# Convolution stage of a two-block decoder kernel: the input normed ahead of its projection, the depthwise taps dealt anew over three engines

## The chip, the cores and the metric

The kernel runs on one core of one Trainium2 chip. The metric is the device time of one execution in microseconds (us), lower is better. A core has five engines that run beside each other, each with a queue of its own: PE (TensorE, matrix products into the eight banks of PSUM), DVE (VectorE, elementwise), ACT (ScalarE, functions and scaled copies), POOL (GpSimd, elementwise on SBUF only) and SP (which here only starts transfers). They meet at semaphores.

## The reference, cut to what matters

A model of three layers is computed for 512 tokens and 1024 channels in float32. The change lies in the first half of the first layer, a convolution module:

```python
def conformer_conv(h, w_pw1, b_pw1, w_dw, b_dw, ln_g, ln_b, w_pw2, b_pw2):
    u = h @ w_pw1 + b_pw1                 # 1024 -> 2048; h = rmsnorm(x, norm_mix[0])
    a, gate = jnp.split(u, 2, axis=-1)
    u = a * jax.nn.sigmoid(gate)
    u = lax.conv_general_dilated(         # causal, 31 taps, each channel for itself
        u, w_dw[:, None, :], window_strides=(1,), padding=[(CONV_WIDTH - 1, 0)],
        dimension_numbers=("NWC", "WIO", "NWC"), feature_group_count=CONV_CHANNELS) + b_dw
    u = jax.nn.silu(layernorm(u, ln_g, ln_b))
    return u @ w_pw2 + b_pw2
```

Behind it follow the gated feed-forward, attention and retention layers, which the change leaves as they are.

## The kernel before

**Tiles.** Channels lie on the 128 partitions, tokens along the free side: `X`, `U` and `CV` are eight tiles (m = 0 to 7) of 128x512. Every weight matrix streams through in units of 256 columns. A float32 unit `W_raw` is split into a rounded part `W_hi` (ACT) and a rest `W_lo` (DVE), and so is the input (`H_hi`, `H_lo`); a product is then three matmuls, lines L627, L628 and L629. The first layer `pw1` has eight units j = 0 to 7 of 8 x 2 products, 48 matmuls each; two units are in flight, in PSUM banks PS0/PS1 and PS2/PS3. Unit j gives one tile of the linear half and one of the gate, and from them DVE makes tile j of `U`.

**The norm.** `H_hi` and `H_lo` hold x times its gain, without the token's factor 1/rms. ACT squares the tiles of `X`, DVE adds the squares up in `SSUM`, PE sums over the partitions (`first_sum`, L686) after three products of unit 1, ACT takes the root, DVE the reciprocal `R4`, PE spreads it over a bank (`token_spread`, L692), ACT copies it to `R`, and every unit's results are multiplied by `R` on DVE (`T_g`, `T_u`; L1970, L1973) before gate and product (`U`, L1976).

**The 31 taps of eight tiles, 248 in all.** PE takes 66 (tile 1, parts of 5 and 7) as three matmuls each with a diagonal matrix of tap weights (`D_hi`, `D_lo`, built on ACT by `diagonals` in chunks of six taps, three chunks ahead). 32 of them stand among the products of units 4 to 7, the rest behind unit 7. They need the tile's split input `UP_hi`, `UP_lo`. DVE takes 124 (tiles 0, 3, 4, 6), one instruction each (L1930), counted out behind each unit by `DVE_TAPS`. POOL takes 58 (tile 2, parts of 5 and 7): ACT writes tap weight times shifted `U` to one of four `TAP` buffers (`scaled_tap`, L1272), and POOL adds it to `CV` (L1752). Each addition waits for the one before, since both go into the same tile. DVE joins the parts of split tiles (`conv_join`).

**Order.** Every engine's order is written by hand. Among PE's taps stand the three products of `bias_products` (L715), which make the attention's bias table. They wait for two small DMAs and for a memset of `table` by POOL (L1774, semaphore `pads_set` at 2). POOL reaches it between its second and third tile:

```python
            taps(1)
            mean_add(3)
            mean_add(4)
            pool.wait_ge(ln_sum, len(MEAN_POOL) - 1)
            pool.wait_ge(acc_ready, 2 * (L.base + L.n))
            nc.gpsimd.memset(table[BUCKETS:BUCKETS + 1, :], NEG).then_inc(pads_set, 1)
            pool.wait_ge(pads_set, 2)
            taps(2)
```

Once all tiles are made, PE sums them over channels (L772 to L778), DVE subtracts the mean (L1997), and the layernorm and layer `pw2` follow.

Of the kernel before, what the change touches and what calls it, by code (L numbers as in the profile page):

```python
# [5 lines left out]
F32 = mybir.dt.float32  # L6
# [4 lines left out]
P = 128  # L11
# [31 lines left out]
SS_ADDS = [7, 7, 7, 7, 7, 5, 7, 5]  # L43
# [6 lines left out]
COPIED_NORMS = [MIX0, FFN_PRE, FFN_POST]  # L50
# [19 lines left out]
POOL_TAPS = [(m, t) for m, end in POOL_TILES for t in range(end)]  # L70
POOL_ENDS = [n + 1 for n, (m, t) in enumerate(POOL_TAPS) if (m, t + 1) in POOL_TILES]
SCALED = [n for n, (m, t) in enumerate(POOL_TAPS) if t]
CHUNK = 6
CHUNKS = (len(PE_TAPS) + CHUNK - 1) // CHUNK
FIRST_TAP, TAPS_INSIDE = 64, 32
CHUNK_AT = {g: c for c, g in enumerate([40, 46, 52] + [FIRST_TAP + 2 * CHUNK * (c - 2) for c in range(3, 8)])}
TAKE_AT = FIRST_TAP + 2 * PE_ENDS[0] + 1
SCALED_AT = [50 + 3 * k // 2 for k in range(30)] + [101 + 3 * k // 2 for k in range(18)]
MEAN_POOL = [0, 2, 3, 1, 4]
MADE = [0, 3, 4, 5, 6, 7]  # L80
# [103 lines left out]
def build(nc, a, out):  # L184
# [13 lines left out]
    with ctx:  # L198
# [99 lines left out]
        TAP = [SQ[:, 0, :], SQ[:, 1, :], STD[:], T_hid[:]]  # L298
# [3 lines left out]
        D_hi = [sb(f"D_hi{i}", [P, CHUNK, P], F32R, at=w_at + 11264 * i + 8192) for i in range(3)]  # L302
        D_lo = [sb(f"D_lo{i}", [P, CHUNK, P], F32R, at=w_at + 11264 * (3 + i) + 8192) for i in range(3)]
        tap_hi = sb("tap_hi", [P, CONV_WIDTH * DT], F32R, at=arena + 68352)
# [70 lines left out]
        acc_free = sem("acc_free")  # L375
        x_ready = sem("x_ready")
# [20 lines left out]
        glu_made = sem("glu_made")  # L397
# [122 lines left out]
        def _(sp):  # L520
# [38 lines left out]

            sp.dma_start(vecs[:, 0:DT], a["vecs"][:, 0:DT]).then_inc(gain_in, 16)  # L560
            sp.dma_start(W_raw[0][:, 0:FIRST_COLS], a["pw1"][0][:, 0:FIRST_COLS]).then_inc(first_in, 16)
            for i in range(4):
                sp.dma_start(X[:, 2 * i:2 * i + 2, :], a["x"][:, 2 * i:2 * i + 2, :]).then_inc(x_in[i], 16)
                if i == 0:
                    sp.dma_start(W_raw[0][:, FIRST_COLS:2 * FIRST_COLS], a["pw1"][0][:, FIRST_COLS:2 * FIRST_COLS]).then_inc(raw_in[0], 16)
# [50 lines left out]
        def _(pe):  # L616
# [65 lines left out]
            def first_sum():  # L682

                pe.wait_ge(ss_made, SS_ADDS[MIX0])
                for b in range(4):
                    last = nc.tensor.matmul(AUX[0][:, b:b + 1], tokens(SSUM, b), ones[:, 0:1], start=(b == 0), stop=(b == 3))  # L686
                last.then_inc(stat_ready, 1)
# [30 lines left out]
            def conv_tap(n):  # L718
# [6 lines left out]
                if n in (0, *PE_ENDS):  # L725
                    pe.wait_ge(u_lo, p + 1)
                    pe.wait_ge(r_copied, COPIED_NORMS.index(MIX0) + 1)
                    if p == 2:
                        pe.wait_ge(conv_pe_taken, 1)
                if x == 0:  # L730
                    pe.wait_ge(diag_made, c + 1)
                d_hi, d_lo = D_hi[c % 3][:, x, :], D_lo[c % 3][:, x, :]
# [5 lines left out]
            L = layers["pw1"]  # L738
            for k in range(L.kt):
# [9 lines left out]
            for j in range(1, L.n):  # L749
# [3 lines left out]
                for half in range(2):  # L753
                    for k in range(L.kt):
                        last = product(j % 2, L.kt, half, k, H_hi, H_lo)
                        if k == L.kt - 1:
                            last.then_inc(acc_ready, 1)
                        g = SLOTS * j + 8 * half + k
                        if g == SUM0_AT:
                            first_sum()  # L760
                        if g == SPREAD0_AT:
                            pe.wait_ge(r_made, MIX0 + 1)
                            token_spread(AUX[1], r_ps)
# [9 lines left out]
            pe.wait_ge(conv_made, MADE.index(5) + 1)  # L773
            nc.tensor.matmul(PS[0][:], ones, CV[:, 5, :], start=False, stop=False)
            pe.wait_ge(conv_made, MADE.index(6) + 1)
            nc.tensor.matmul(PS[0][:], ones, CV[:, 6, :], start=False, stop=False)
            pe.wait_ge(conv_made, MADE.index(7) + 1)
            nc.tensor.matmul(PS[0][:], ones, CV[:, 7, :], start=False, stop=True).then_inc(ln_sum_ready, 1)  # L778
# [394 lines left out]
        def _(act):  # L1173
            act.dma_start(cmat[:, 0:2, :], a["cmat"][:, 0:2, :]).then_inc(const_in, 16)
            act.wait_ge(gain_in, 16)
# [55 lines left out]

            warm_table(ACT.Sqrt)
            act.wait_ge(first_in, 16)
            nc.scalar.activation(W_hi[0][:, 0:FIRST_COLS], W_raw[0][:, 0:FIRST_COLS], ACT.Copy).then_inc(w_half, 1)
            for m in range(0, DT, 2):
                if m == 2:
# [1428 lines left out]
```

## Time and profile before

| | |
|---|---|
| time, median of 3 runs | 1810.86 us (1808.42 to 1811.15) |
| the profiled execution | 1810.43 us, of it span 1808.7 us |
| PE busy | 1743.7 us (96%) |
| DVE, ACT, POOL busy | 1017.8, 716.0, 249.1 us |
| first matmul of `pw1` | 9.61 us |
| PE's longest pause in the stage | 12.1 us, up to 141.99 us |
| first instruction of the layernorm (L1997) | 170.60 us |

The span goes from the first to the last instruction; 1.73 us of the time lie outside it. Times in the trace are counted from the start of the span. The convolution stage ends at 170.60 us; all that follows hangs on that point and is the same program in both kernels. A matmul's own duration (0.39 us) overlaps the next one; what it takes of PE is the distance from one start to the next.

### The profile page before, as it was taken

Reading aid. Unit: us, or ns where it says so; the run is one execution under the profiler, and the core shown is the slowest. Engines: PE = TensorE matmul, PEld = TensorE weight load, DVE = VectorE, ACT = ScalarE, POOL = GpSimd, SP = SyncE. Lnnn points to the kernel's source line nnn. Section 1 sums busy time; section 2 is a strip of 40 time slices with the busy share of each in tenths; the row PEclk is TensorE's granted clock in tenths of the full one; section 3 lists DMA queues with packets and bytes.
Section 4 is the critical chain, followed back from the end, with each engine's and each line's share of the span. In section 5 each row is a group of like instructions: output and inputs, shape, how many; then the busy total and the mean of one; then the engine's idle time right before and its main releaser. Section 6 shows DMA issues by size and latency. Waiting matters only on the chain.

```text
span 1808.7 us, 20938 instructions
## 1 busy us (share of the span) xinstructions
PE 1743.7 (96%) x7984; PEld 1385.3 (77%) x7984; DVE 1017.8 (56%) x1268; ACT 716.0 (40%) x1064; POOL 249.1 (14%) x183
## 2 busy tenths in 40 slices
PE   7987899999999999999999999989999999999997
PEld 6874788888888777788888888756557778888886
DVE  6898664423444556654434434559856677537753
ACT  5776532312233344432212233464554454324431
POOL 0783110000001000100000004572200200000001
PEclk9998899999999999999999999999999899999998
DMA  5220322322232311222322232423202122322221
GB/s 182 70 70 11 115 93 93 119 99 73 98 120 75 121 71 53 86 95 93 128 70 93 96 125 82 146 75 112 80 32 78 62 93 101 119 70 93 101 97 47
DMA packets 28052, 164.62 MB, mean 91 GB/s; under 512 B 4511, under 2 KB 5675, under 8 KB 11596
## 3 DMA queue, kind: packets, MB, share of 16 engines
q1 hardware_dynamic: 25088, 158.11, 25.1%
q10 hardware_dynamic: 2892, 5.55, 1.0%
q8 instruction: 46, 0.75, 0.2%
q14 instruction: 26, 0.21, 0.0%
HBM read 156.28 MB, written 4.47 MB: 89 GB/s over the span
## 4 chain that ended last, share of the span: by engine, by line
PE 80%; DVE 10%; POOL 5%; ACT 3%; issue 2%; DMA 0%; POOLq 0%; DVEq 0%; SPq 0%; ACTq 0%
PE PS L627 25%; PE PS L628 25%; PE PS L629 25%; POOL CV L1752 4%; DVE PS L1930 2%; DVE W_lo L1880 2%; ACT W_hi L1169 1%; DVE WK L2320 1%; DVE SSUM L2361 1%; DVE TOP L2318 1%; PE PS L1060 1%; PE PS L1071 1%; POOL ISC L1824 1%; DVE PS L2497 0%; DVE X L2500 0%
## 5 line engine op out<-in xcount | busy, mean ns | idle before, releaser
L627 PE MATMUL PS<-H_hi,W_hi 128*128 128x512 f32 x1600 | 641.6, 401 | 17.8 <-DVE H_lo L1860 13.5
L629 PE MATMUL PS<-H_hi,W_lo 128*128 128x512 f32 x1600 | 626.0, 391 | 0.0
L628 PE MATMUL PS<-H_lo,W_hi 128*128 128x512 f32 x1600 | 625.8, 391 | 0.0
L1169 ACT ACTIVATE W_hi<-W_raw 128x2048 fp32r<-128x2048 f32 (+2 forms) x130 | 262.6, 2020 | 674.7 <-PE PS L629 674.7
L627 PEld LDWEIGHTS PS<-H_hi,W_hi 128*128 128x128 f32 x1600 | 301.9, 189 | 105.5 <-issue 41.1
L1880 DVE TENSOR_TENSOR W_lo<-W_raw,W_hi 128x2048 fp32r<-128x2048 f32 (+2 forms) x130 | 332.3, 2556 | 59.4 <-ACT W_hi L1169 59.1
L629 PEld LDWEIGHTS PS<-H_hi,W_lo 128*128 128x128 f32 x1600 | 301.8, 189 | 64.5
L628 PEld LDWEIGHTS PS<-H_lo,W_hi 128*128 128x128 f32 x1600 | 302.2, 189 | 58.9 <-issue 1.2
L627 PE MATMUL PS<-HID_hi,W_hi 128*128 128x512 f32 x640 | 250.7, 392 | 7.5 <-DVE HID_lo L2016 7.4
L1727 POOL TENSOR_TENSOR SSUM<-SSUM,SQ 128x512 f32<-128x512 f32 x43 | 63.6, 1480 | 1353.7 <-ACT SQ L1211 1352.3
L629 PE MATMUL PS<-HID_hi,W_lo 128*128 128x512 f32 x640 | 250.0, 391 | 0.0
L628 PE MATMUL PS<-HID_lo,W_hi 128*128 128x512 f32 x640 | 249.9, 391 | 0.0
L627 PEld LDWEIGHTS PS<-HID_hi,W_hi 128*128 128x128 f32 x640 | 120.8, 189 | 34.1 <-issue 8.5
L629 PEld LDWEIGHTS PS<-HID_hi,W_lo 128*128 128x128 f32 x640 | 120.7, 189 | 25.3
L628 PEld LDWEIGHTS PS<-HID_lo,W_hi 128*128 128x128 f32 x640 | 120.9, 189 | 24.8
L2058 DVE TENSOR_TENSOR T_u<-PS,R 128x512 f32<-128x512 f32 x44 | 30.4, 691 | 156.1 <-PE PS L629 156.1
L2066 DVE TENSOR_TENSOR T_hid<-T_u,T_act 128x512 f32<-128x512 f32 x66 | 45.7, 693 | 81.1 <-ACT T_act L1410 78.5
L2031 DVE TENSOR_TENSOR X<-X,PS 128x512 f32<-128x512 f32 x40 | 27.0, 684 | 113.9 <-PE PS L629 113.7
L1930 DVE SCALAR_TENSOR_TENSOR PS<-U,vecs,PS 128x512 f32<-128x512 f32 x112 | 75.5, 752 | 0.2
L1418 ACT ACTIVATE HID_hi<-T_hid 128x512 f32 (+1 forms) x66 | 42.0, 636 | 57.7 <-DVE T_hid L2066 57.7
L1860 DVE SCALAR_TENSOR_TENSOR H_lo<-X,vecs,H_hi 128x512 fp32r<-128x512 f32 x40 | 36.2, 914 | 27.3 <-ACT H_hi L1196 27.2
L2072 DVE TENSOR_TENSOR HID_lo<-T_hid,HID_hi 128x512 f32 (+1 forms) x66 | 45.2, 684 | 1.4 <-ACT HID_hi L1418 1.4
(300 smaller groups left out, 1493.5 us busy)
## 6 DMA issues: line engine op xcount, KB each, us to landing
W_raw<-in_inp SPq DMA_DIRECT2D x13, 1024.0 KB, 4.8
W_raw<-in_pw SPq DMA_DIRECT2D x11, 1024.0 KB, 4.8
W_raw<-in_gu0a SPq DMA_DIRECT2D x11, 1024.0 KB, 4.8
W_raw<-in_gu0b SPq DMA_DIRECT2D x11, 1024.0 KB, 4.8
W_raw<-in_gu1a SPq DMA_DIRECT2D x11, 1024.0 KB, 4.8
W_raw<-in_gu1b SPq DMA_DIRECT2D x11, 1024.0 KB, 4.8
W_raw<-in_gu2a SPq DMA_DIRECT2D x11, 1024.0 KB, 4.8
W_raw<-in_gu2b SPq DMA_DIRECT2D x11, 1024.0 KB, 4.7
```

The lines of the kernel that those rows point to most:

```text
L627: nc.tensor.matmul(dst[:], wh, x_hi[:, k, :], start=(k == first), stop=False)
L628: nc.tensor.matmul(dst[:], wh, x_lo[:, k, :], start=False, stop=False)
L629: return nc.tensor.matmul(dst[:], wl, x_hi[:, k, :], start=False, stop=(k == last))
L1169: nc.scalar.activation(W_hi[b][:, 0:n], W_raw[b][:, 0:n], ACT.Copy).then_inc(w_hi, 1)
L1418: nc.scalar.activation(dst, T_hid[:], ACT.Copy).then_inc(hid_hi_made, 1)
L1727: nc.gpsimd.tensor_tensor(SSUM[:], SSUM[:], SQ[:, m.parity, :], ALU.add).then_inc(ss_made, 1)
L1752: nc.gpsimd.tensor_tensor(CV[:, m, :], CV[:, m, :], TAP[k % len(TAP)], ALU.add).then_inc(pool_tap, 1)
L1860: nc.vector.scalar_tensor_tensor(out=dst, in0=src, scalar=scale, in1=hi, op0=ALU.mult, op1=ALU.subtract).then_inc(h_lo_made, 1)
L1880: nc.vector.tensor_tensor(W_lo[b][:, 0:n], W_raw[b][:, 0:n], W_hi[b][:, 0:n].bitcast(F32), ALU.subtract).then_inc(w_lo, 1)
L1930: i = nc.vector.scalar_tensor_tensor(out=dst, in0=src, scalar=w, in1=acc, op0=ALU.mult, op1=ALU.add)
L2066: nc.vector.tensor_tensor(T_hid[:], T_u[:], T_act[:], ALU.mult).then_inc(hid_made, 1)
L2072: nc.vector.tensor_tensor(HID_lo[:, k, :].rearrange("p o n -> p (o n)"), T_hid[:], hi, ALU.subtract).then_inc(hid_lo_made, 1)
```

## The change

Six things are altered, all up to the layernorm.

1. **The norm goes first.** `X` is loaded before the weights, over two queues. ACT squares it. PE sums each squared tile as it comes (`first_sums`, 8 x 4 products with one column), in place of DVE's additions and `first_sum`. Root, reciprocal and spread follow, then DVE multiplies `X` by the spread factor into `CV` (`normed`), and `H_hi` and `H_lo` are made of that. Only then does unit 0 begin.
2. **Gates from PSUM.** Sigmoid reads the gate's bank, the product the other bank; the two multiplications by `R` per unit are gone.
3. **Order of PE.** All eight units run without taps between them, then 54 taps: tile 4 whole, tile 6 from tap 8. `bias_products` stands behind tap 24, not 55.
4. **POOL's tiles.** 1 and 5 whole, 6 up to tap 7. Each has two sums, `CV` and a new tile `CV2`, taken in turn, so that an addition waits for the one before the last; one more addition joins them.
5. **Buffers.** Eleven `TAP` buffers for four, four chunks of diagonals for three.
6. **DVE** takes tiles 0, 2, 3 and 7 (again 124 taps), 12 behind each of units 0 to 6 and 40 behind unit 7.

```diff
-PE_TILES = [(1, 0), (5, 22), (7, 5)]
+PE_TILES = [(4, 0), (6, 8)]
-DVE_TILES = [0, 3, 4, 6]
-DVE_TAPS = [5, 8, 9, 16, 16, 16, 16]
-POOL_TILES = [(2, CONV_WIDTH), (5, 22), (7, 5)]
+DVE_TILES = [0, 2, 3, 7]
+DVE_TAPS = [12] * 7
+POOL_TILES = [(1, CONV_WIDTH), (5, CONV_WIDTH), (6, 8)]
+PRODUCTS_WITH = [0, 8, 7, 7, 7, 8, 8, 8]
+CHUNKS_WITH = {0: [0, 1], 2: [2], 4: [3]}
...
+            def first_sums():
+
+                for m in range(DT):
+                    pe.wait_ge(sq_made, m + 1)
+                    for b in range(4):
+                        last = nc.tensor.matmul(AUX[0][:, b:b + 1], tokens(FIRST_SQ[m], b), ones[:, 0:1],
+                                                start=(m == 0 and b == 0), stop=(m == DT - 1 and b == 3))
                 last.then_inc(stat_ready, 1)
...
             L = layers["pw1"]
+            first_sums()
+            pe.wait_ge(r_made, MIX0 + 1)
+            token_spread(AUX[1], r_ps)
...
-                        if g >= FIRST_TAP and g % 2 == 0:
-                            conv_tap((g - FIRST_TAP) // 2)
-            for n in range(TAPS_INSIDE, len(PE_TAPS)):
+            for n in range(len(PE_TAPS)):
                 conv_tap(n)
-                if n == 55:
+                if n == 24:
                     bias_products()
...
+            for j in range(L.n):
+                glu_gate(j)
+                if j < L.n - 1:
+                    split_hi(act, L, At(j))
+                scaled_taps(PRODUCTS_WITH[j] // 2)
+                if j - 1 in (4, 6):
+                    conv_hi((j - 1) // 2 - 2)
+                for c in CHUNKS_WITH.get(j, []):
+                    diagonals(c)
+                scaled_taps(PRODUCTS_WITH[j] - PRODUCTS_WITH[j] // 2)
...
-                    pool.wait_ge(pool_tap, n)
-                    nc.gpsimd.tensor_tensor(CV[:, m, :], CV[:, m, :], TAP[k % len(TAP)], ALU.add).then_inc(pool_tap, 1)
+                    pool.wait_ge(pool_tap, n - 1)
+                    nc.gpsimd.tensor_tensor(acc, acc, TAP[k % len(TAP)], ALU.add).then_inc(pool_tap, 1)
...
             taps(1)
             mean_add(3)
-            mean_add(4)
             pool.wait_ge(ln_sum, len(MEAN_POOL) - 1)
             pool.wait_ge(acc_ready, 2 * (L.base + L.n))
             nc.gpsimd.memset(table[BUCKETS:BUCKETS + 1, :], NEG).then_inc(pads_set, 1)
...
+            def normed(m):
+
+                if m == 0:
+                    dve.wait_ge(r_ps, TOKEN_NORMS.index(MIX0) + 1)
+                nc.vector.tensor_tensor(CV[:, m, :], X[:, m, :], AUX[1][:], ALU.mult).then_inc(xn_made, 1)
...
+            normed(0)
+            normed(1)
             dve.wait_ge(w_half, 1)
             nc.vector.tensor_tensor(W_lo[0][:, 0:FIRST_COLS], W_raw[0][:, 0:FIRST_COLS],
                                     W_hi[0][:, 0:FIRST_COLS].bitcast(F32), ALU.subtract).then_inc(first_lo, 1)
...
-                nc.vector.tensor_tensor(T_g[:], PS[2 * b + 1][:], R[:], ALU.mult).then_inc(gate_in, 1)
...
-                nc.vector.tensor_tensor(T_u[:], PS[2 * b][:], R[:], ALU.mult).then_inc(acc_free, 1)
...
-                nc.vector.scalar_tensor_tensor(out=U[:, j, HALO:HALO + SEQ], in0=T_u[:], scalar=vec("b_pw1", j),
-                                               in1=T_act[:], op0=ALU.add, op1=ALU.mult).then_inc(glu_made, 1)
+                nc.vector.scalar_tensor_tensor(out=U[:, j, HALO:HALO + SEQ], in0=PS[2 * (j % 2)][:], scalar=vec("b_pw1", j),
+                                               in1=GATE[j % 2][:], op0=ALU.add, op1=ALU.mult).then_inc(glu_made, 1)
```

The names in the rows of the programs below carry buffer numbers: `PS0` to `PS3` are the units' banks, `PS4` is `AUX[0]`, `PS5` is `AUX[1]`, `SQ`, `T_g`, `T_u`, `T_act`, `T_hid` and `R` hold squares at first and tap products later, and `cmat` holds the constant matrices. What stands in brackets is what an instruction waits for.

On PE the statistics of the norm stood inside unit 1, the sum first:

```order
L628 MATMUL PS2<-H_lo_51,W_hi1_55 128x512
L629 MATMUL PS2<-H_hi_50,W_lo1_57 128x512
L686 MATMUL PS4<-cmat_58,SSUM_64 128x1 [waits ss_made]
L686 MATMUL PS4<-cmat_58,SSUM_64 128x1 x3
L627 MATMUL PS2<-H_hi_50,W_hi1_55 128x512
```

Now PE's program begins with them, one group for each squared tile:

```order
L691 MATMUL PS4<-cmat_58,SSUM_64 128x1 [waits sq_made,const_in]
L691 MATMUL PS4<-cmat_58,SSUM_64 128x1 x3
L691 MATMUL PS4<-cmat_58,SQ_65 128x1 [waits sq_made]
L691 MATMUL PS4<-cmat_58,SQ_65 128x1 x3
...
L691 MATMUL PS4<-cmat_58,R_62 128x1 [waits sq_made]
L691 MATMUL PS4<-cmat_58,R_62 128x1 x3
L698 MATMUL PS5<-cmat_58,R4_72 128x128 [waits r_made]
L698 MATMUL PS5<-cmat_58,R4_72 128x128 x3
```

Four one-column matmuls became 32, and they and the spread stand ahead of the first dense product.

Further down on PE, behind unit 7, the bias products now stand after tap 24, the first tap of the fifth chunk of diagonals:

```order
L739 MATMUL PS4<-UP_hi_141,D_lo3_150 128x512
L737 MATMUL PS4<-UP_hi_141,D_hi0_143 128x512 [waits diag_made]
L738 MATMUL PS4<-UP_lo_142,D_hi0_143 128x512
L739 MATMUL PS4<-UP_hi_141,D_lo0_147 128x512
L721 MATMUL PS1<-onehot_101,table_102 4x384 [waits const2_in,acc_free,pads_set,tab_in]
L721 MATMUL PS2<-onehot_101,table_102 4x384
L721 MATMUL PS3<-onehot_101,table_102 4x384
L737 MATMUL PS4<-UP_hi_141,D_hi0_143 128x512
```

29 taps come behind that wait; before, 10 did.

On POOL, the memset that this wait names stood behind the 22 taps of POOL's second tile:

```order
L1752 TENSOR_TENSOR CV_77<-CV_77,STD_63 128x512 [waits pool_tap,act_scaled]
L1762 TENSOR_TENSOR SSUM_64<-SSUM_64,CV_77 128x512 [waits ln_sum,conv_pe_taken]
L1762 TENSOR_TENSOR SSUM_64<-SSUM_64,CV_77 128x512 [waits ln_sum,conv_made]
L1774 MEMSET table_102 1x12 [waits acc_ready,ln_sum]
L1746 TENSOR_SCALAR CV_77<-U_76,vecs_59 128x512 [waits glu_made,vec_in,pads_set]
```

Now it stands behind all 31 taps and the joining addition (L1753) of the second tile:

```order
L1758 TENSOR_TENSOR CV_77<-CV_77,STD_63 128x512 [waits pool_tap,act_scaled]
L1753 TENSOR_TENSOR CV_77<-CV_77,CV2_140 128x512 [waits pool_tap]
L1765 TENSOR_TENSOR SSUM_64<-SSUM_64,CV_77 128x512 [waits ln_sum,conv_made]
L1776 MEMSET table_102 1x12 [waits acc_ready,ln_sum]
L1748 TENSOR_SCALAR CV_77<-U_76,vecs_59 128x512 [waits acc_free,pool_tap,vec_in,pads_set]
```

POOL has ten more instructions ahead of it than before on tile 5, and one fewer addition to `SSUM`.

## Rows read from the trace of the kernel before

**Rows 1.** Timeline of the start: start us, duration us, engine, line, operation.

```profile
6.41 1.06 ACT L1234 ACTIVATE W_hi<-W_raw 128x1024 fp32r<-128x1024 f32 x1 [3.40 <-DMA W_raw<-in_pw]
9.61 0.77 PE L627 MATMUL PS<-H_hi,W_hi 128*128 128x512 f32 x1 [9.61 <-DVE H_lo L1860]
10.31 1.33 ACT L1196 ACTIVATE H_hi<-X,vecs 128x512 fp32r<-128x512 f32 x2 [0.30 <-DMA X<-in_x]
22.84 0.39 PE L627 MATMUL PS<-H_hi,W_hi 128*128 128x512 f32 x1
```

**Rows 2.** Timeline of PE, ACT and DVE around the first norm's statistics.

```profile
24.89 0.95 PE L686 MATMUL PS<-cmat,SSUM 128*128 128x1 f32 x8
26.30 0.18 DVE L1964 RECIPROCAL R<-STD 128x4 f32<-128x4 f32 x1 [3.13 <-ACT STD L1222]
28.55 1.05 PE L692 MATMUL PS<-cmat,R 128*128 128x128 f32 x8
35.69 0.50 PE L627 MATMUL PS<-H_hi,W_hi 128*128 128x512 f32 x1
```

**Rows 3.** Windows (length; PE, PEld, DVE, ACT, POOL busy; clock) and a later norm's spread.

```profile
9.60:14.40 4.80, 4.79 (x11) 3.78 (x12) 4.67 (x7) 4.50 (x9) 0.00 (x0) 1.00 1.03 402
1416.00:1417.00 1.00, 0.95 (x10) 0.87 (x9) 0.99 (x2) 1.00 (x3) 0.00 (x0) 1.00 0.00 0
1417.00:1418.00 1.00, 1.00 (x8) 1.00 (x8) 0.89 (x1) 0.75 (x1) 0.00 (x0) 0.66 0.00 0
1418.89 2.08 PE L692 MATMUL PS<-cmat,R 128*128 128x128 f32 x8 [0.57 <-DVE R L2486]
1794.23 3.49 PEld L692 LDWEIGHTS PS<-cmat,R 128*128 128x128 f32 x16 [0.65 <-DVE R L2486]
```

**Rows 4.** Timeline of POOL and DVE among the units.

```profile
52.06 0.77 POOL L1746 TENSOR_SCALAR CV<-U,vecs 128x512 f32<-128x512 f32 x1 [50.95 <-DVE U L1976]
60.96 2.72 POOL L1752 TENSOR_TENSOR CV<-CV,SQ 128x512 f32<-128x512 f32 x2
65.26 1.74 POOL L1752 TENSOR_TENSOR CV<-CV,T_hid 128x512 f32<-128x512 f32 x1
67.14 4.82 POOL L1752 TENSOR_TENSOR CV<-CV,SQ 128x512 f32<-128x512 f32 x2
68.51 2.29 DVE L1880 TENSOR_TENSOR W_lo<-W_raw,W_hi 128x2048 fp32r<-128x2048 f32 x1
90.36 7.99 DVE L1930 SCALAR_TENSOR_TENSOR PS<-U,vecs,PS 128x512 f32<-128x512 f32 x12
```

**Rows 5.** Timeline of POOL elsewhere: additions and products that need not wait for their predecessor.

```profile
1146.77 1.29 POOL L1811 TENSOR_TENSOR KK<-KK,CS 128x512 f32<-128x512 f32 x1 [25.45 <-DVE CS L2288]
1148.02 1.29 POOL L1812 TENSOR_TENSOR TSK<-TSK,CS 128x512 f32<-128x512 f32 x1
```

**Rows 6.** Timeline of the stage's end: PE, POOL and DVE.

```profile
141.99 0.79 PE L734 MATMUL PS<-UP_hi,D_hi 128*128 128x512 f32 x1 [12.11 <-DVE UP_lo L1951]
148.93 0.10 POOL L1774 MEMSET table<- 1x12 f32 x1
155.85 2.10 PE L715 MATMUL PS<-onehot,table 33*4 33x384 f32 x6
165.00 1.02 PE L772 MATMUL PS<-SSUM,cmat 128*128 128x512 f32 x2
165.87 1.02 PE L774 MATMUL PS<-CV,cmat 128*128 128x512 f32 x2
169.54 1.02 PE L778 MATMUL PS<-CV,cmat 128*128 128x512 f32 x2
170.60 4.88 DVE L1997 SCALAR_TENSOR_TENSOR CV<-PS,CV 128x512 f32<-128x512 f32 x8 [1.36 <-PE PS L778]
```

**Rows 7.** Windows around PE's restart, columns as in the windows above.

```profile
142.00:147.20 5.20, 5.20 (x12) 4.12 (x13) 5.13 (x8) 5.20 (x15) 4.86 (x4) 0.50 0.02 5
147.20:165.00 17.80, 17.80 (x73) 12.91 (x72) 17.80 (x28) 13.40 (x34) 7.60 (x8) 0.99 0.01 2
```

More of the change, by code:

```diff
@@ L59 @@
 RET_HEADS = 8
-PE_TILES = [(1, 0), (5, 22), (7, 5)]
+PE_TILES = [(4, 0), (6, 8)]
 PE_TAPS = [(m, t) for m, t0 in PE_TILES for t in range(t0, CONV_WIDTH)]
 PE_ENDS = [n + 1 for n, (m, t) in enumerate(PE_TAPS) if t == CONV_WIDTH - 1]
-DVE_TILES = [0, 3, 4, 6]
-DVE_TAPS = [5, 8, 9, 16, 16, 16, 16]
-POOL_TILES = [(2, CONV_WIDTH), (5, 22), (7, 5)]
[L70 to L73, printed above, removed]
-CHUNKS = (len(PE_TAPS) + CHUNK - 1) // CHUNK
[L75 to L80, printed above, removed]
+DVE_TILES = [0, 2, 3, 7]
+DVE_TAPS = [12] * 7
+POOL_TILES = [(1, CONV_WIDTH), (5, CONV_WIDTH), (6, 8)]
+POOL_STEPS = [(m, t) for m, end in POOL_TILES for t in range(end + 1)]
+POOL_ENDS = [n + 1 for n, (m, t) in enumerate(POOL_STEPS) if (m, t) in POOL_TILES]
+SCALED = [n for n, (m, t) in enumerate(POOL_STEPS) if t >= 2 and (m, t) not in POOL_TILES]
+CHUNK, CHUNK_BUFS = 6, 4
+CHUNKS = (len(PE_TAPS) + CHUNK - 1) // CHUNK
+PRODUCTS_WITH = [0, 8, 7, 7, 7, 8, 8, 8]
+CHUNKS_WITH = {0: [0, 1], 2: [2], 4: [3]}
+MEAN_POOL = [0, 1, 2, 3]
+MEAN_PE = [4, 5, 7, 6]
+MADE = [0, 2, 3, 7, 6]
 def dilated_jobs():
@@ L680, in token_sum @@
                 last.then_inc(stat_ready, 1)
[L682 to L686, printed above, removed]
+            def first_sums():
[4 more added lines that the diff above has]
+                                                start=(m == 0 and b == 0), stop=(m == DT - 1 and b == 3))
                 last.then_inc(stat_ready, 1)
@@ L772, in _ @@
             nc.tensor.matmul(PS[0][:], ones, SSUM[:], start=True, stop=False)
[L773 to L778, printed above, removed]
+            for m in MEAN_PE:
+                if m == 4:
+                    pe.wait_ge(conv_pe_taken, 1)
+                elif m == 5:
+                    pe.wait_ge(pool_tap, POOL_ENDS[1])
+                else:
+                    pe.wait_ge(conv_made, MADE.index(m) + 1)
+                last = nc.tensor.matmul(PS[0][:], ones, CV[:, m, :], start=False, stop=(m == MEAN_PE[-1]))
+            last.then_inc(ln_sum_ready, 1)
             pe.wait_ge(fvec_made, 3)
@@ L1881, in lo_of, with normed_lo @@
                                         ALU.subtract).then_inc(w_lo, 1)
+            def normed(m):
+                if m == 0:
+                    dve.wait_ge(r_ps, TOKEN_NORMS.index(MIX0) + 1)
+                nc.vector.tensor_tensor(CV[:, m, :], X[:, m, :], AUX[1][:], ALU.mult).then_inc(xn_made, 1)
+            def normed_lo(m):
+                dve.wait_ge(h_hi_made, m + 1)
+                nc.vector.scalar_tensor_tensor(out=H_lo[:, m, :], in0=CV[:, m, :], scalar=vec("norm_mix0", m),
+                                               in1=H_hi[:, m, :].bitcast(F32), op0=ALU.mult, op1=ALU.subtract).then_inc(h_lo_made, 1)
+            dve.wait_ge(std_made, MIX0 + 1)
+            nc.vector.reciprocal(R4[:], STD4[:]).then_inc(r_made, 1)
+            for m in range(4):
+                dve.wait_ge(x_in[m], 16)
+            normed(0)
+            normed(1)
             dve.wait_ge(w_half, 1)
@@ L1885, in _ @@
                                     W_hi[0][:, 0:FIRST_COLS].bitcast(F32), ALU.subtract).then_inc(first_lo, 1)
[L1886 to L1898 removed]
+            dve.wait_ge(gain_in, 16)
+            for m in range(DT):
+                normed_lo(m)
+                if m < DT - 2:
+                    normed(m + 2)
+                if m == 3:
                     dve.wait_ge(w_hi, 1)
```

202 lines of the change are left out of this document (77 added, 125 removed).

## The prediction

> **What bounds the kernel now.** PE is busy nearly throughout, so a change pays only where PE pauses or where it does work that another engine could do. I read the timeline of the start first; it shows PE beginning at 9.61 us, when the first split inputs are there [rows 1]. The timeline of the stage's end shows the one long pause, 12.1 us up to 141.99, and then a second limit: PE's last tap ends at 165.00, but the sum over channels ends only with the product at 169.54, because DVE's last tiles come late, and the layernorm starts at 170.60 [rows 6]. This 170.60 is what I compute anew; everything behind it is the same program in both kernels and I let it keep its length.
>
> So the stage has a PE path and a path through POOL, ACT and DVE. The change lightens PE's (54 taps for 66) and starts it later. I follow it in five steps.
>
> **Step 1, the start: PE begins about 17 us later.** Before, PE's first need is half a weight unit and two tiles of X. After, it is the whole norm. The first squared tile can be there at about 6.9 us: before, the first transfer of that size was used at 6.41 [rows 1], X is now issued ahead of it, say 6.3, and the square adds 0.6. Then come 32 one-column matmuls. Each float32 matmul of this kind is two rows (four gave x8 [rows 2]), so 64. At the high clock eight take 0.95 us, about 0.10 each [rows 2]. But PE is not at the high clock at the start: its first products start 0.43 us apart (11 in 4.8 us [rows 3]), as after the pause (12 in 5.2 at a granted clock of 0.50 [rows 7]), later ones 0.23. The column of the granted clock says 1.00 there all the same, so I go by the distances, which are those of the 1.2 GHz level. And one-column matmuls do not bring the clock up: at the later norm PE was busy with them through 1416 to 1418, and the granted clock fell from 1.00 to a mean of 0.66 in the second of these microseconds; the spread behind took 2.08 where it had taken 1.05 [rows 2, 3]. At that level 16 weight loads of the spread took 3.49 us, 0.21 each [rows 3]. 64 x 0.213 = 13.6 us, so the sums end at 20.5; the squares are long done (before, as many bytes as all of X has had landed when the tile of 10.31 was used [rows 1]; the last square ends near 11.4). From the end of the sums to the spread 0.7 us (from 25.84 to the reciprocal at 26.30, its 0.18 and a semaphore [rows 2]), the spread 2.1 at the low level [rows 3], two `normed` 1.2, half a unit's `W_lo` 1.1, `H_lo` and its semaphore 0.9: PE starts at 26.6, **17.0 us later than 9.61**. Bounds: 0.10 for each row makes it 9.5 us later (then the squares, ready at 11.4, set the pace), 0.233 makes it 18.3. I take 0.213, the row of the same matrix loads at the same level.
>
> **Step 2, the units.** Unit 0 took 22.84 - 9.61 = 13.2 us, cold start included [rows 1], so it ends at 39.8. Unit 1 took 35.69 - 22.84 = 12.85 with the two groups of statistics inside; 48 x 0.2275 = 10.9 without [rows 1, 2]. Unit 1 ends at 50.7, unit 7 at 116.2. Does anything hold them? DVE per unit: product 0.65, `W_lo` 2.2, twelve taps 7.9 [rows 4], together 10.8, with two joins and a split of `U` 78 us over seven units against 76 of PE. It is level with PE, falls behind by some us, and has a whole unit's slack, since PE needs the banks of unit j back only at unit j + 2. ACT's gate, `W_hi`, seven or eight tap products and a chunk of diagonals fit into a unit too, if only just. The multiplications by `R` (16 x 0.6 on DVE) were hidden, and their removal costs and pays nothing on PE's path.
>
> **Step 3, POOL.** It starts with U of tile 1. Unit 0's product is made 1.5 us after its end, then `W_lo` up to 4.9 and twelve taps up to 12.9, then unit 1's product: 39.8 + 13.6 = 53.4 (52.06 before [rows 4]). From there to the memset of `table` stand:
> - 58 additions with their predecessor but one as condition. Dependent ones followed each other at 1.43 (2.72 for two with 1.29 each [rows 4]); independent ones at 1.25 [rows 5]. I take 1.26: 73.1 us.
> - 4 tap products of POOL's own at 0.75: 3.0. Two joins and three additions to `SSUM`, dependent, at 1.43: 7.2.
> - Blocks by DVE. Where DVE makes a `W_lo`, POOL's addition takes 2.1 us longer (4.82 for two at 67.14, against 2.72, `W_lo` at 68.51 [rows 4]). Six of them fall into the stretch, 12.5, and two splits of `U` at 0.6, 1.2.
>
> Sum 97.0 us: **the memset is done at 53.4 + 97.0 + 0.2 = 150.6**, where it was at 148.93 [rows 6]. The product into `U` also held POOL up before, by 0.44 (1.74 against 1.30 [rows 4]); it read two tiles of SBUF. It now reads one of PSUM, like the taps, beside which POOL's additions kept 1.29. I charge nothing; at the old price it would be 7 x 0.44 = 3 us.
>
> The Trainium skill, GPSIMD Engine Reference, section Key points, says that GpSimd contends with VectorE instructions that have two SBUF inputs. By that rule the product no longer blocks, and the trace agrees for `W_lo` (2.1 us) and for the taps (none). Charging only by this rule or by the old row makes 0 or 3 us.
>
> **Step 4, the wait that moved.** PE reaches tap 24 at 116.2 + 24 x 0.695 = 132.9 and finishes it at 133.6 (three products of 0.232 a tap). Then `bias_products` wants `pads_set` at 2, the memset at 150.6. Before, the same wait stood behind tap 55 at 155.85, after the memset at 148.93, and cost nothing [rows 6]. **Now PE waits 17 us**, and 29 taps are queued behind. ACT's chunks up to the eighth are built meanwhile; its last needs tap 30 and follows in time.
>
> **Step 5, the end.** After the pause PE is at 1.2 GHz for some 5.2 us, as from 142.0 to 147.2 (granted clock 0.50 [rows 7]). The bias products took 2.0 high [rows 6], so 3.85; three more products low, 1.3; the other 84 of the 29 taps 19.5. Sum 24.65, so PE's taps end at 175.3. The sums over channels go from 165.00 to 169.54 plus 1.02 now; without the wait for DVE five follow each other at 0.87 [rows 6], and the layernorm starts 4.5 us behind the last tap: **179.8 instead of 170.60, 9.2 us later**. POOL's remaining eight taps (12 us behind the memset) and DVE's forty (done near 154) are hidden by PE's 24.65. If that cover were gone, nothing earlier than PE's own end would be.
>
> In one sum: start 26.6, unit 0 13.2, seven units 76.4, 25 taps 17.4, wait 17.0, bias products, 29 taps and cold clock 24.65, sums 4.5: 179.8, against 170.60 it is +9.2. The profiled execution took 1810.43 us, 0.43 under the median, so I forecast 1810.43 + 9.2 = **1819.6 us**. Since PE waits for POOL, a delay of the start goes through POOL's path one to one, and an error of 0.02 in POOL's distance is 1.2 us. The forecast's own range is 1815 to 1824.
>
> **Rivals.**
> - *The start's sums run fast.* If PE's clock rises under them, then after the 4.8 us that the first products needed the other 42 rows take 0.10: sums end near 16, the spread takes 1.05, the first unit starts warm. The start comes 7.7 us sooner: +1.5, 1811.9. For it: PE is busy without a gap. Against it: so it was from 1416 to 1418, and the clock fell [rows 3]. Chance 0.13. The Trainium skill, TensorE: Matmul & The Clock Gate, Part 1, says that the clock follows how busy PE has been lately; taken as busy time alone this is that rival, and rows 3 disagree.
> - *Two sums do not loosen POOL.* If the addition still follows at 1.43, as with a fixed cost for any semaphore of its own, step 3 grows by 58 x 0.17 = 9.9 us: 1829.5. For it: no addition of before waits on its predecessor but one. Against it: independent ones stand at 1.25 with waits of other kinds [rows 5]. Chance 0.12.
> - *Faster: the two sums overlap on POOL.* If of 1.29 us much is latency that two chains hide, the distance could approach that of POOL's one-input product, 0.77 [rows 4]. At 0.77 the memset is at 122, before PE asks at 133.6; PE ends its taps at 116.2 + 37.5 + 2.0 = 155.7, the layernorm starts at 160.2, and the time is 1800. It decides against slower below 1.04, where the memset comes before 138. For it: nothing but the shape of the change. Against it: 1.25 between independent ones. Chance 0.05.
> - *The pauses are worse.* A late tap product holds ACT, that the gate, that DVE, and PE loses part of a unit: 2 to 6 us on top, up to 1826. ACT reaches the ring's end in unit 6. Chance 0.08.
>
> **How the numbers follow.** Forecast 0.62, rivals 0.13, 0.12, 0.05, 0.08. The range 1811.5 to 1826 holds the forecast, the fast start and the worse pauses, and leaves out the 1.43 and the overlap, 0.17. Within 0.2% (3.6 us, about what a measurement of this kernel can tell from no change) lie the fast start and the forecast's lower edge, 0.17; faster, the overlap and what a fast start and shorter blocks would make together, 0.06; slower the rest, 0.77.
>
> **What the profile after would show.** Step 1: 64 rows of one-column products up to about 20.5 and the first dense product near 26.6. Step 2: unit 7's last product near 116 with no gap. Step 3: POOL's additions 1.26 apart, longer by 2.1 at each `W_lo`, memset near 150.6. Step 4: PE idle before the bias products for about 17 us. Step 5: a low clock behind it and the layernorm near 180. The prediction is wrong if the sums take under 10 us, if the additions stand at 1.43 or under 1.04, or if PE does not wait at the bias products.

## The result, and the profile after

The changed kernel takes 1826.33 us (median of 5 runs, 1820.75 to 1827.58), the kernel before beside it 1810.70 (1807.52 to 1811.15): a ratio of 1.0085, 95% interval 1.0073 to 1.0096, so it is slower by 15.6 us. The forecast was 1819.6 with a range of 1811.5 to 1826. The profiled execution took 1827.28 us with a span of 1825.5.

The five times are not spread evenly: two lie at 1820.75 and 1821.51, three at 1826.33, 1827.28 and 1827.58. The experiments show what parts them. The median falls into the upper group by three runs to two; with one run fewer there it would have been near 1821.

The start, in the timeline (start us, duration, engine, line, operation, what ended the idle time before it). It answers to [rows 1, 2]:

```profile
7.61 1.87 PE L691 MATMUL PS<-cmat,SSUM 128*128 128x1 f32 x8 [7.61 <-DMA cmat<-in_cmat]
...
19.58 1.85 PE L691 MATMUL PS<-cmat,R 128*128 128x1 f32 x8
...
21.99 2.08 PE L698 MATMUL PS<-cmat,R 128*128 128x128 f32 x8 [0.57 <-DVE R L1897]
...
27.43 0.76 PE L631 MATMUL PS<-H_hi,W_hi 128*128 128x512 f32 x1 [3.36 <-DVE H_lo L1893]
```

Eight groups of eight rows stand 1.71 us apart, 0.213 a row, from 7.61 to 21.43; in the kernel before, PE went on to the next product 0.81 us after the first of eight such rows at 24.89, 0.10 a row [rows 2]. The 0.213 is the distance of the 1.2 GHz level, although the column of the granted clock says 1.00 here, as it does in [rows 3]. The first dense product is at 27.43.

POOL, and DVE behind the units; this answers to [rows 4, 6]:

```profile
59.33 2.54 POOL L1758 TENSOR_TENSOR CV<-CV,SQ 128x512 f32<-128x512 f32 x2
61.83 1.29 POOL L1758 TENSOR_TENSOR CV<-CV,STD 128x512 f32<-128x512 f32 x1
63.09 1.28 POOL L1758 TENSOR_TENSOR CV<-CV,T_hid 128x512 f32<-128x512 f32 x1
...
111.48 0.83 DVE L1959 TENSOR_TENSOR UP_lo<-U,UP_hi 128x542 fp32r<-128x542 f32 x1
125.65 23.93 DVE L1959 TENSOR_TENSOR UP_lo<-U,UP_hi 128x542 fp32r<-128x542 f32 x1 [1.47 <-ACT UP_hi L1289]
149.07 1.63 POOL L1753 TENSOR_TENSOR CV<-CV,CV 128x512 f32<-128x512 f32 x1
155.53 0.69 DVE L1944 TENSOR_TENSOR CV<-CV,PS 128x512 f32<-128x512 f32 x1
156.30 1.27 POOL L1765 TENSOR_TENSOR SSUM<-SSUM,CV 128x512 f32<-128x512 f32 x1 [5.60 <-DVE CV L1944]
157.62 0.10 POOL L1776 MEMSET table<- 1x12 f32 x1
```

The additions start 1.25 us apart, and each lasts 1.29: there is no gap between them. One instruction stands out. `UP_lo`, a subtraction of two tiles in SBUF, takes 0.83 us for tile 4 and 23.93 us for tile 6. The 0.83 us is about what the work takes, so the second one stood still for some 23 us; below, such an instruction is called held. It ends at 149.58, when POOL has come to the merge of its two sums (149.07), the first operation of the stretch that waits for its direct predecessor. Queued behind `UP_lo` on DVE are the last nine taps of tile 3. POOL's addition of tile 3 waits for them 5.60 us, and the memset of `table` stands behind that addition.

PE at the same place:

```profile
157.82 4.00 PE L721 MATMUL PS<-onehot,table 33*4 33x384 f32 x6 [22.77 <-issue]
...
184.40 1.02 PE L770 MATMUL PS<-SSUM,cmat 128*128 128x512 f32 x2
...
188.89 3.68 DVE L1984 SCALAR_TENSOR_TENSOR CV<-PS,CV 128x512 f32<-128x512 f32 x6 [3.55 <-PE PS L778]
```

PE stood still for 22.77 us. The trace names no releaser, but the program waits there for `pads_set`, and the memset ended 0.10 us earlier. The layernorm starts at 188.89 where it had started at 170.60 [rows 6]: +18.29, against a difference of 16.85 between the two profiled times. So what follows the start of the layernorm did not keep its length, though its program is the same: 1638.1 us before, 1636.6 after, and from 1633.5 to 1638.1 over all profiles of this case. Why is open; a few us of a time can come from there. Windows behind the pause (length; PE, PEld, DVE, ACT, POOL busy; granted clock; DMA):

```profile
157.80:162.00 4.20, 4.17 (x7) 0.87 (x8) 4.20 (x7) 0.00 (x0) 4.16 (x4) 0.50 0.00 0
162.00:166.00 4.00, 4.00 (x10) 3.13 (x11) 4.00 (x7) 0.00 (x0) 4.00 (x4) 0.50 0.00 0
```

The granted clock is 0.50, the 1.2 GHz level, and the distance of the products falls from 0.43 to 0.23 only at 166.9, 9 us after 157.8, where it had been some 5 us behind the shorter pause of before [rows 7].

### The profile page after: what moved, and what is told of

Its sections match the earlier page's. It is cut to its first block, busy times and chain, and to the rows that moved or that the text cites. A ratio compares the mean times of both kernels' runs of the same rounds, so it can differ in the third digit from the quotient of the medians.

```text
span 1825.5 us, 20914 instructions
## 1 busy us (share of the span) xinstructions
PE 1749.4 (96%) x8006; PEld 1392.0 (76%) x8006; DVE 1028.8 (56%) x1251; ACT 713.1 (39%) x1047; POOL 266.8 (15%) x197
## 4 chain that ended last, share of the span: by engine, by line
PE 87%; DVE 7%; issue 2%; ACT 2%; POOL 1%; DMA 0%; ACTq 0%; DVEq 0%; POOLq 0%
PE PS L631 27%; PE PS L633 26%; PE PS L632 26%; DVE W_lo L1881 1%; PE PS L691 1%; PE PS L737 1%; PE PS L738 1%; PE PS L739 1%; DVE WK L2307 1%; DVE SSUM L2348 1%; DVE TOP L2305 1%; PE PS L1061 1%; ACT W_hi L1170 1%; PE PS L1072 1%; POOL ISC L1826 0%
## 5 line engine op out<-in xcount | busy, mean ns | idle before, releaser
L1861 DVE SCALAR_TENSOR_TENSOR H_lo<-X,vecs,H_hi 128x512 fp32r<-128x512 f32 x32 | 30.6, 957 | 27.6 <-ACT H_hi L1198 27.5
```

The lines of the kernel that those rows point to most:

```text
L1861: nc.vector.scalar_tensor_tensor(out=dst, in0=src, scalar=scale, in1=hi, op0=ALU.mult, op1=ALU.subtract).then_inc(h_lo_made, 1)
```

## The experiments

My theory: three things make the loss. (a) The bias products' wait now stands ahead of 29 taps, so PE's pause is on the path. (b) POOL's additions without a gap hold back a DVE instruction with two inputs in SBUF (`UP_lo` or a `W_lo`), which delays the memset further in a part of the runs. (c) The start is late through 64 one-column rows at the low clock. The rivals are in the expectations. Times are medians; each batch has its own runs of the kernel before.

**First batch** (before: 1809.41, 23 runs).

*Bias products behind the last tap.*

```
-                if n == 24:
+                if n == 53:
                     bias_products()
```

> The bias products stand behind the last tap instead of behind tap 24; nothing else is changed. Theory: PE's pause at tap 24 is gone, its taps end at 134.8 + 29 x 0.695 = 155.0, but UP_lo is still held for some 24 us, so the memset stays near 157.6 and DVE's taps of tile 7 still end near 177.5, and now they set the end: layernorm near 180.4 instead of 188.9, the time 8.5 us under the changed kernel, about 1818. Rival A (the pause is worth all of its 22.8 us, DVE's late tiles catch up when PE is not in the way): layernorm near 164, time near 1802. Rival B (what was lost at the start is the whole loss and the pause was hidden by DVE anyway): time unchanged, 1826.

Measured: 1806.13 (12 runs): nine between 1802.38 and 1806.40, three at 1820.56, 1822.23 and 1823.61. Against the kernel before this is no difference (ratio 1.0004, interval 0.9981 to 1.0028). In the profiled run (1802.38) the case that no theory had named occurred: `UP_lo` took 1.74 us, and with it short the layernorm starts at 166.56:

```profile
125.08 1.74 DVE L1959 TENSOR_TENSOR UP_lo<-U,UP_hi 128x542 fp32r<-128x542 f32 x1 [1.45 <-ACT UP_hi L1289]
...
163.32 0.69 DVE L1952 TENSOR_TENSOR CV<-CV,PS 128x512 f32<-128x512 f32 x1 [8.55 <-POOL CV L1753]
166.56 4.88 DVE L1984 SCALAR_TENSOR_TENSOR CV<-PS,CV 128x512 f32<-128x512 f32 x8 [2.55 <-PE PS L778]
```

The one wait's place was worth about 16 us (1821 to 1805) where nothing is held, and the same program holds the instruction in one run and not in another.

*POOL lets UP_lo in at one place.*

```
+                    if (m, t) == (5, 13):
+                        pool.wait_ge(u_lo, 2)
                     pool.wait_ge(act_scaled, k + 1)
```

> GpSimd waits once, ahead of its addition for tap 13 of tile 5, until VectorE's UP_lo of tile 6 is done; nothing else is changed. Theory (GpSimd's additions, which follow each other without a gap, keep VectorE's two-input instruction out of SBUF): UP_lo takes about 0.8 to 1.5 us instead of 23.9, GpSimd loses up to 1.5 us at the wait, tile 3 is made near 133, GpSimd no longer waits for it, the memset is at 151.2 instead of 157.6, the layernorm 6.4 us sooner, time near 1821, and the runs lie closer together than the changed kernel's 7 us. Rival (UP_lo was late for another reason, for instance a transfer or ScalarE's writes, or its record is wrong): UP_lo still long or the memset still near 157.6, time near 1826.

Measured: four of six runs at 1821.23 to 1822.18 as expected, two at 1838.99 and 1840.45, which it had not foreseen. In the profiled run (1821.46) the memset is at 151.37, PE's pause 16.8 and the layernorm at 182.86:

```profile
124.68 1.74 DVE L1961 TENSOR_TENSOR UP_lo<-U,UP_hi 128x542 fp32r<-128x542 f32 x1 [1.45 <-ACT UP_hi L1289]
151.37 0.10 POOL L1778 MEMSET table<- 1x12 f32 x1
151.57 3.99 PE L721 MATMUL PS<-onehot,table 33*4 33x384 f32 x6 [16.84 <-issue]
```

`UP_lo` took 1.74 us, as without the wait in the run above, so this run alone does not show that the wait is what made it short.

*The memset ahead of the addition that waits for tile 3.*

```
-            mean_add(3)
-            pool.wait_ge(ln_sum, len(MEAN_POOL) - 1)
+            pool.wait_ge(pool_tap, POOL_ENDS[1])
             pool.wait_ge(acc_ready, 2 * (L.base + L.n))
             nc.gpsimd.memset(table[BUCKETS:BUCKETS + 1, :], NEG).then_inc(pads_set, 1)
             pool.wait_ge(pads_set, 2)
+            mean_add(3)
+            pool.wait_ge(ln_sum, len(MEAN_POOL) - 1)
```

> GpSimd's memset of the table stands ahead of the addition that waits for tile 3; nothing else is changed. Theory: UP_lo is held as before, about 24 us, but it reaches the end only through tile 3, that addition and the memset; so the memset comes at 150.9, the pause is 6.7 us shorter and the time near 1820.5, although VectorE's taps still end near 177. Rival (the late VectorE costs the time by itself, by tile 7 or by its product): under 2 us gained, time near 1825.

Measured: 1819.69, all five runs between 1818.71 and 1820.55. The profile has the memset at 149.99, the pause at 15.6 and `UP_lo` at 1.74, so the time agrees, but what the edit does beside a held `UP_lo` was not seen. The memset comes 1.4 us sooner than in the experiment before it (151.37), where nothing was held either; that much is the addition that it has passed.

*The start's squares added on DVE, one sum on PE.*

```
-                for m in range(DT):
-                    pe.wait_ge(sq_made, m + 1)
-                    for b in range(4):
+                pe.wait_ge(ss_made, SS_ADDS[MIX0])
+                for b in range(4):
...
```

Behind the cut, DVE gets its seven additions of squares back.

> The squares are added on VectorE as in the kernel before and TensorE makes one sum of 4 one-column products instead of 32; the norm still stands ahead of the projection. Theory: 8 rows at 0.213 take 1.7 us behind the last addition near 11.1, so the sums end near 12.9 instead of 21.4 and the first dense product starts 8.5 us sooner, near 18.9; all that follows moves with it, time near 1818. Rival (something else holds the first product: weights, transfers, or a clock that is lower because PE had less to do before): the first product under 5 us sooner and the time above 1821.

Measured: 1813.28 (12 runs) in three groups: seven between 1811.08 and 1813.31, two at 1816.92 and 1818.33, three near 1830. The sum's rows start at 12.45, the first dense product stands at 20.29, 7.1 us sooner than 27.43. Expected were 8.5 sooner, but DVE's last addition ended near 12.3, not 11.1. The profiled run, 1816.92, has `UP_lo` at 23.94. Against the changed kernel's runs in the same condition (1827.28 with `UP_lo` held, 1821 without) the start is worth 10.4 and about 9 us, more than 7.1: the first dense products stand 0.43 apart until 23.8 here (3.5 us), and until 33.5 in the changed kernel (6.1 us), and the second unit's product into `U` comes at 45.78 instead of 54.16, 8.4 sooner. The layernorm comes 9.0 sooner, at 179.85; the remaining 1.4 of the 10.4 lie behind it or outside the span.

**Second batch** (before: 1808.23, 17 runs).

*Both: bias products last, and the wait for UP_lo.*

> The bias products behind the last tap, and GpSimd waits once, ahead of tap 13 of tile 5, for VectorE's UP_lo of tile 6. Theory (the runs of the first of these edits alone that lie 17 us over its others are those in which UP_lo is held for 24 us): with the wait they are gone, all runs between 1802 and 1807. Rival (another of VectorE's two-input instructions, a W_lo of the units, is held in some runs, as GpSimd's additions follow one another without a gap there too): a part of the runs still lies some 17 us higher, although UP_lo is short in every one.

Measured: 1805.87 (12 runs), ten between 1802.84 and 1806.81, two at 1823.26 and 1823.93. That is the rival's sign: `UP_lo` of tile 6 cannot be the cause here, since POOL waits for it. What the two high runs held, no profile of this kernel shows; the single runs below show the same 17 to 18 us in another kernel, from one `W_lo`.

*Every addition waits for its predecessor.*

```
-                    pool.wait_ge(pool_tap, n - 1)
+                    pool.wait_ge(pool_tap, n)
```

> Every addition of GpSimd waits for its predecessor, as in the kernel before, instead of for its predecessor but one; the two running sums stay. Theory: the additions stand 1.43 apart, with a gap in which VectorE's two-input instructions always get in, so no instruction of VectorE takes over 4 us and the runs lie within 4 us of each other; the price is up to 58 x 0.17 = 9.9 us on GpSimd's way to the memset (161 against 151.2 of the runs without a held instruction), time near 1831. Rival (the high runs come from something else, for instance transfers at the start): still runs 6 and 17 us over the others.

Measured: 1832.40, four runs within 0.55 us. `UP_lo` takes 0.72 us, no `W_lo` over 2.96, the memset is at 161.85 and the layernorm at 193.47.

*Every third waits for its predecessor.*

```
-                    pool.wait_ge(pool_tap, n - 1)
+                    pool.wait_ge(pool_tap, n - (t % 3 > 0))
```

> Of GpSimd's additions those of every third tap wait for their predecessor, the others for their predecessor but one. Theory: a gap of 0.17 us every 3.9 us is enough to let VectorE in; no instruction of VectorE takes over 6 us, the runs lie within 4 us of each other; the price is 20 gaps, 3.5 us: time near 1824.5, between the changed kernel's lower runs (1821) and the kernel with all additions dependent (1831). Rival (a single gap is not enough, VectorE gets in only by luck): runs still 6 or 17 us over the others.

Measured: 1825.24, five runs within 1.74 us; `UP_lo` 0.72, no `W_lo` over 3.08, memset at 154.71. Both prices came as expected, and no run of either kernel lies apart from the others.

*Bias products last, the start's additions, every third dependent.*

> Three edits together: bias products behind the last tap, the start's squares added on VectorE with one sum on TensorE, and every third addition of GpSimd waiting for its predecessor. Theory: the layernorm started at 166.56 with the first edit alone in a run without a held instruction, set by GpSimd's way to tile 6; the start gives 7.1 back, the gaps take 3.5: layernorm near 163, against 170.60 of the kernel before, time near 1801 (the runs of the first edit alone: 1802 to 1806, less 3.6), and no run far above the others. Rival (the sum over channels is set by something that does not move with the start): within 2 us of the first edit alone, 1805.

Measured: **1798.26 us (1797.01 to 1798.55), ratio 0.9942 to the kernel before, interval 0.9929 to 0.9955.** The layernorm starts at 161.03, 9.6 us ahead of [rows 6], and waits for POOL's last merge. Behind the layernorm this profile is 4.6 us shorter than that of before (1633.5 against 1638.1), for which no run here shows a cause. The three causes add up: 1826.3 less 16 (a), 6 (b) and 9 (c), plus 3.9 for the gaps, makes 1799.

```profile
119.24 0.72 DVE L1962 TENSOR_TENSOR UP_lo<-U,UP_hi 128x542 fp32r<-128x542 f32 x1 [3.07 <-ACT UP_hi L1287]
159.13 0.69 DVE L1955 TENSOR_TENSOR CV<-CV,PS 128x512 f32<-128x512 f32 x1 [11.21 <-POOL CV L1751]
161.03 4.87 DVE L1987 SCALAR_TENSOR_TENSOR CV<-PS,CV 128x512 f32<-128x512 f32 x8 [1.22 <-PE PS L776]
```

**Third batch** (before: 1808.64, 21 runs). Where are the gaps needed?

```
-                    pool.wait_ge(pool_tap, n - 1)
+                    pool.wait_ge(pool_tap, n - (0 if t % 3 == 0 and (m, t) < (5, 8) else 1))
+                    pool.wait_ge(pool_tap, n - (0 if t % 3 == 0 and (m, t) > (5, 9) else 1))
```

> Bias products behind the last tap; every third addition waits for its predecessor only while the dense units run (tile 1 and tile 5 up to tap 7), and behind them there is the one wait for UP_lo. Theory (the runs 17 us over the others are those in which one of the W_lo of the units is held): none of the runs lies high; the time is that of the kernel with the wait alone, 1805.5, plus 11 gaps of 0.17, near 1807. Rival (the held instruction is elsewhere, or the high runs come from the start): one run in four or five still lies near 1824.

> Bias products behind the last tap; every third addition waits for its predecessor only behind the units (tile 5 from tap 10), none before. Theory: UP_lo is short, the W_lo of the units can still be held, so one run in four or five lies near 1823; the others near 1806.5. Rival (what is held is behind the units): all runs within 1803 to 1808.

Both kernels have the bias products behind the last tap. Of the two added lines above, the first is in the first kernel, with the wait for `UP_lo`, and gives gaps while the units run; the second is in the second kernel and gives gaps behind them. Measured: 1807.93 (11 runs within 1.45 us) and 1806.33 (11 runs, 1803.19 to 1806.83). The first time is what the theory said, but in the second kernel it expected two or three high runs and there was none. At the rate of the kernel with the wait alone, 2 in 13 with the single run below, eleven runs without one come about one time in six, for either kernel: the pair does not tell where the gaps are needed.

*Two single runs, each profiled.*

> Bias products behind the last tap and the one wait for UP_lo, once more, for one profile. One run in five or so should lie near 1823; if this is one, the theory expects one W_lo of VectorE among the units to take over 14 us and PE to pause behind it, the rival no instruction of VectorE over 4 us.

> Bias products behind the last tap alone, once more, for one profile. If the run lies near 1820, the theory expects UP_lo or one W_lo of VectorE to take over 14 us; if near 1805, none over 4 us.

The first gave 1806.80 and decides nothing. The second was a high run, 1820.77 us:

```profile
125.06 24.03 DVE L1959 TENSOR_TENSOR UP_lo<-U,UP_hi 128x542 fp32r<-128x542 f32 x1 [1.46 <-ACT UP_hi L1289]
...
180.91 4.87 DVE L1984 SCALAR_TENSOR_TENSOR CV<-PS,CV 128x512 f32<-128x512 f32 x8 [3.15 <-PE PS L778]
```

Its program is that of the first experiment. There a held `UP_lo` had been expected to put the layernorm at 180.4, and here it stands at 180.91.

**Four more single runs** of the two kernels that had the highest group.

> The one wait for UP_lo of tile 6 alone, once more, for one profile. If the run lies near 1839, the theory expects another of VectorE's instructions with two inputs in SBUF (UP_lo of tile 4 or a W_lo of units 3 to 7) to take 10 us or more and PE to pause behind it; the rival expects none over 4 us and the time lost elsewhere. If near 1821, nothing is decided.

> The same kernel and the same expectation as in the look before it.

> The start's additions on VectorE alone, once more, for one profile. Near 1830: the theory expects UP_lo of tile 4 or a W_lo held for 10 us or more; near 1817: UP_lo of tile 6 held for 24 us; near 1812: no instruction over 4 us. The rival expects a run near 1830 with none over 4 us.

> The same kernel and the same expectation as in the look before it.

The first two gave 1820.66 and 1822.22 and decide nothing. The other two gave 1830.06 and 1832.46, and both profiles show the same. From the first of them, DVE and POOL, then PE's waits (us in total, times, longest):

```profile
57.51 22.96 DVE L1879 TENSOR_TENSOR W_lo<-W_raw,W_hi 128x2048 fp32r<-128x2048 f32 x1
80.40 4.03 DVE L1941 SCALAR_TENSOR_TENSOR PS<-U,vecs,PS 128x512 f32<-128x512 f32 x6
...
72.19 6.13 POOL L1756 TENSOR_TENSOR CV<-CV,TAP 128x512 f32<-128x512 f32 x5
97.14 2.55 POOL L1756 TENSOR_TENSOR CV<-CV,SQ 128x512 f32<-128x512 f32 x2 [18.82 <-ACT SQ L1277]
```

```profile
PE PS L719 <- issue: 16.9, 1, 16.9
PE PS L631 <- DVE W_lo L1879: 14.7, 1, 14.7
```

One `W_lo` of the units took 22.96 us instead of 2.3. It ends at 80.47, 2.15 us behind the end of POOL's last addition of the row at 78.32, which is about its own length. POOL stopped there because ACT, which waits for PE, which waits for this `W_lo`, no longer supplied products. PE's pause of 14.7 us comes on top of the one at the bias products. In the profiled run of the same program at 1816.92 us the same `W_lo` got in after one addition, though it came at the same point behind the start of an addition of POOL, 0.17 us (first the held run, then the other):

```profile
57.34 1.30 POOL L1756 TENSOR_TENSOR CV<-CV,R 128x512 f32<-128x512 f32 x1
...
57.21 1.30 POOL L1756 TENSOR_TENSOR CV<-CV,R 128x512 f32<-128x512 f32 x1
57.38 3.28 DVE L1879 TENSOR_TENSOR W_lo<-W_raw,W_hi 128x2048 fp32r<-128x2048 f32 x1
```

## Why the prediction was wrong

**Step 1, the start: right, 0.8 us off.** The rows took 0.213 each, as chosen, and the rival of a rising clock did not occur. The sums began 0.7 us later than the 6.9 I gave, not for the squares (from 5.57) but for the constant matrix `cmat`, which I had not followed.

**Step 2, the units: PE was not stopped, as said, but the step was 1 us too short.** I took unit 0 with the cold start of before, 4.8 us; here the products stood 0.43 apart for 6.1. POOL started at 55.19 for 53.4, 0.8 of it from step 1. PE did not wait between 27.4 and tap 24, which was done at 135.05 for 133.6.

**Step 3, POOL: its own sum right, a wait for DVE left out. This is the step that failed.** The additions stood 1.25 apart (1.26 charged), and where nothing was held the memset came at 151.37, for 150.6. The rival "two sums do not loosen POOL" fell; the kernel with all additions dependent gave what it would have been, 1832. The failed terms are "three additions to `SSUM`, dependent, at 1.43", which hold no wait for the tile that is added, and "Blocks by DVE", which prices what a two-input instruction of DVE costs POOL and not what POOL then costs DVE. In the profiled run `UP_lo` was held for 23.93 us, DVE made tile 3 late, and POOL's addition of tile 3 waited 5.60 us. The memset came at 157.62, 7.0 us behind the forecast: 1.8 from POOL's later start, 5.2 from the stretch up to the memset (102.4 us for 97.2). Step 5's "DVE's forty are hidden" held even so: they ended at 176.8 instead of near 154, while PE's taps went on up to 184.4.

The Trainium skill, GPSIMD Engine Reference, section Key points, which I weighed there, names this contention without saying who waits. The Trainium skill, SBUF — State Buffer, section "SBUF: two separate sides", says that the two engines take a shared pair of ports as an exclusive lock, for a whole instruction, and that the one that comes second waits. The traces agree as to POOL, 2 us for a `W_lo`, and as to the 12 DVE instructions below that waited for one addition. They do not agree for a held one: `UP_lo` stayed out through 18 additions that started after it. In the trace of before every addition of POOL was followed by a gap of 0.14 (1.43 against 1.29 [rows 4]), and each `W_lo` of DVE in that stretch started in such a gap and took its 2.29 us. The change took just these gaps away.

**Step 4, the moved wait: right in kind, and in size where nothing was held** (16.8 for 17). With `UP_lo` held it was 22.8. Moving it to the end of the taps gave about 16 us back where nothing was held.

**Step 5, the end: 1.9 us short.** The bias products took their 3.9 (3.85 forecast), the sums their 4.5, but 87 tap products took 22.65 for 20.8. I had taken the length of the low clock, 5.2 us, from a pause of 12.1 with dense products behind it; behind pauses of 16.8 to 22.8 us, with the bias products first, it was about 9. Which of the two differences made it longer no run tells.

**All steps together.** In one sum for the profiled run: memset +7.0, its landing on PE +0.2, low clock +1.9 make 188.9 from 179.8. Without the held instruction the same steps gave 182.86 and 1821 us, inside the forecast's own range. That they did is in part luck: the layernorm was 3.1 us later than forecast, and what follows it was 1.3 us shorter than before, where I had let it keep its length. And that the median fell outside the range, by 0.3 us, hangs on three of five runs lying in the upper group (one of them is profiled, with the held `UP_lo`); the missing wait in step 3 does not hang on it. The rival "the pauses are worse" had the place (a late product, then everything queued behind) but another mechanism.

What is shown: that a `W_lo` or `UP_lo` is held for 23 to 24 us while POOL's additions follow one another, and ends when POOL stops or comes to a dependent operation, is in five profiles (the changed kernel, the start's additions alone, and three single runs). Without gaps 13 of 58 runs lay 14 us or more above the lowest of their kernel, and 5 more some 6 us. With gaps at every addition or every third, 14 runs of three kernels had none apart; at the rate of 18 in 58 that comes about one time in 180. The two kernels with fewer gaps had none in 22 runs.

The profiles also show which instructions are at risk. In the twelve profiles without gaps, 17 of DVE's two-input instructions (always the same `W_lo`, at 65.76 in the changed kernel, and `UP_lo` of tile 6 where POOL does not wait for it) started 0.13 to 0.18 us behind the start of an addition. Five of the 17 were held; the other 12 lost about 1.0 us. The 62 that started later in an addition, or while POOL paused, lost at most 0.62 us.

What is not shown: what decides between held and free for those 17, which started at the same point. And why the gaps help: in the profiles with gaps at every addition or every third, no such instruction started 0.13 to 0.18 us behind an addition. So the gap may be what lets DVE in, or the gaps may only have moved the moment at which DVE asks. No run keeps the moment and adds the gap.

## What to carry to other kernels

Before making an engine's stream gapless, list the instructions of the other engine that need what the stream occupies, and who is queued behind them: the 0.14 us between dependent additions looked like waste, and it was where DVE's instructions had started. One dependent operation in three kept about two thirds of the gain (3.9 of 11.1 us given up), and none of its 10 runs lay apart. Where the times of one program fall into groups, take a profile of a run from each group before naming a cause. And when work is reordered, move each wait to just ahead of the first reader of its result: one line was worth 16 us here, as much as the whole loss.

## What the runs showed of the hardware

A VectorE instruction with two inputs in SBUF can stand still for 23 to 24 us (0.7 and 2.3 us of work) beside GpSimd additions that start every 1.25 us and last 1.29, in some runs of a program and not in others. Those that did had started 0.13 to 0.18 us behind the start of an addition (5 of 17); of the 62 that started later or in a pause none did. GpSimd additions of 128x512 that wait for their direct predecessor start 1.43 us apart, those that wait for the one before it 1.25. VectorE's taps, with one input in SBUF and one in PSUM, kept 0.66 us each beside the same stream. One-column products with their weight loads stood 0.213 us apart for 13.8 us without a pause, and the dense products behind them 0.43 us apart for 6.1 us more, the distances of the 1.2 GHz level. After a pause of 22.8 us TensorE's clock stayed at 1.2 GHz (granted clock 0.50) for 9 us of work, 3.9 of it products of 33 rows by 384, against 5 us after 12.1.
